# Hybrid encoder trunk: intra-chunk products in narrower column tiles, and reloads of spilled projections issued by SyncE

## The chip, the cores and the metric

The kernel runs on one core of one Trainium2 chip. The metric is the device time of one execution in microseconds (us). TensorE (PE) multiplies, VectorE (DVE) and ScalarE (ACT) read its results from PSUM, GpSimd (POOL) and SyncE (SP) do the rest. SP and ACT issue DMAs, each on a queue of its own.

## What is computed

Two layers of a bidirectional mixer over 512 + 256 tokens of width 1024, all in float32. Each layer has a gated linear attention branch (GLA, 4 heads, 128 channels for the key) and a grouped-query attention branch; both read one normalised input through one projection, are gated, projected, merged and projected again. The change touches the inner part of GLA. For one head and one direction it is

```python
def step(S, inp):
    qi, ki, vi, gi = inp
    b = jnp.cumsum(gi, axis=2)
    diff = b[:, :, :, None, :] - b[:, :, None, :, :]
    decay = jnp.exp(jnp.where(mask[None, None, :, :, None], diff, -jnp.inf))
    A = jnp.einsum('bhic,bhjc,bhijc->bhij', qi, ki, decay)
    o = (jnp.einsum('bhij,bhjv->bhiv', A, vi)
         + jnp.einsum('bhic,bhcv->bhiv', qi * jnp.exp(b), S))
```

with `g = log_sigmoid(h @ w_gate + b_gate) / 16`, run forward and, strictly, backward, and summed. The decay differs for each channel, so `A` isn't one product of two scaled matrices.

## The kernel before

**Levels.** The kernel builds the decayed token-by-token matrix of a head by doubling spans. `LEVELS` is 1, 2, 4 to 256. Step n = 0 gives the diagonal (no decay). Step n >= 1 has span `LEVELS[n - 1]`: it pairs each block of `span` tokens with its neighbour block, with queries and keys scaled by the decay to the border between the two. TensorE multiplies keys (stationary) by queries (moving) into PSUM, VectorE copies the entries that belong to this level into `amat` under a mask (`collect`, L1712; for n = 0 a plain copy of everything, L1710), and scales queries, keys and block totals for the next span (`doubled`, L1696, L1698, L1702). ScalarE merges the two scaled rows of keys into one (`merge_k`, L1064). An entry outside the mask of a level is never read from that level. A head has ten steps, n = 0 to 9; there are four heads in each of two layers, so eight heads in all.

**Shape of the products.** Steps 1 to 6 (spans 1 to 32) run as 12 matmuls of 64 by 64 at L733, each writing half of PSUM's partitions; steps 0, 7 and 8 run as six of 128 by 128 at L728; step 9 as four at L716. All are plain float32, and the trace shows each of them as two MATMUL rows (12 for six matmuls, 24 for twelve).

**What fills the time between.** While VectorE and ScalarE work on a level, TensorE runs `background`: the input projection of the columns that are needed later, three float32r matmuls (L585 to L587) for each token tile and k block, so many tiles for each step by the table `GLA_DONE` (mostly 11 tiles, 33 matmuls). Every finished 256-column group is copied by ScalarE to `stg` (L956) and stored to DRAM (`proj`, L973), 18 groups in each layer. Each matmul with w_hi and w_lo needs a weight block that SP has loaded (L493), that ScalarE has rounded (`split`, L941) and GpSimd has subtracted (L1431), in a ring of four slots. ScalarE's split stays three blocks ahead of TensorE, and SP's load one block further.

**Heads.** On TensorE the first three heads of a layer are one hardware loop (`at.repeat`), whose waits compare with register values and whose n = 0 product has a computed address; the fourth is written out.

**Reloads.** The stored groups come back by DMAs that ScalarE issues between its own work (`fetch`, L982), each 768 KB: in the fourth head one `q` or `kv` group in each step (`fetch_qk`), each followed one step later by ScalarE's squares of it (L1086); after the attention groups four of `zb` and four of `ma`; later four of `mb`. ScalarE's program is in order, so what stands behind an issue waits until the issue is over. `zb` and `ma` take the place of `act_lo` and `act_hi`, which the last background products read.

Of the kernel before, what the change touches and what calls it, by code (L numbers as in the profile page):

```python
# [58 lines left out]
CHUNK = 64  # L59
AH, KVH, DH = 16, 4, 64  # L60
# [55 lines left out]
for done, n in zip(ATT_DONE, ATT_PIECE):  # L116
# [22 lines left out]
        "w_lo_done": 8},  # L139
    "sync gla background": {  # L140
        "w_lo_done": 16},
    "sync rope background": {
        "w_lo_done": 8},
    "sync attention background": {
        "w_lo_done": 16},
    "sync gla branch": {
        "w_lo_done": 8},
    "sync attention branch": {
        "w_lo_done": 8},
# [76 lines left out]
class Semaphores:  # L226


    def __init__(self, nc):
# [21 lines left out]
        self.qkv_in = sem("qkv_in")  # L251
# [80 lines left out]
def trunk(nc, x_prompt, x_sample, norm_g, w_in, w_gate_f, b_gate_f, w_gate_b, b_gate_b, gla_norm_g,  # L332
# [139 lines left out]
    with nc.Block() as block:  # L472

        @block.sync
        def _(sp):
            at = Counts("sync", sp)
# [10 lines left out]
            def load_group(w, layer, col, width=HALF, blocks=KT):  # L487
                ld = w.shape[2]
                for k in range(blocks):

                    sp.wait_ge(s.w_lo_done, at("w_lo_done"))
                    src = bass.AP(w.tensor, layer * (D * ld) + col + k * P * ld, [[ld, P], [1, width]])
                    sp.dma_start(w_raw[:, k % RING, 0:width], src).then_inc(s.w_slot[k % RING], 16)  # L493

            def load_output(layer):

                for _ in range(2):
                    for i in range(2 * KT):
                        sp.wait_ge(s.w_lo_done, at("w_lo_done"))
                        src = bass.AP(w_out.tensor, layer * (D * D) + i % 2 * HALF + i // 2 * P * D, [[D, P], [1, HALF]])  # L500
                        sp.dma_start(w_raw[:, i % RING, :], src).then_inc(s.w_slot[i % RING], 16)

            for layer in range(DEPTH):
# [6 lines left out]
                with at.repeat(GH, "gla background") as h:  # L510
                    for i in range(2):
                        load_group(w_in, layer, h * (2 * BGW) + C_QB + BGW + i * BGW, BGW)
                load_group(w_in, layer, C_ZB + 3 * BGW, BGW)
# [5 lines left out]
                for w, name in ((w_branch_a, "gla branch"), (w_branch_b, "attention branch")):  # L519
                    with at.repeat(2, name) as g:  # L520
                        load_group(w, layer, g * HALF)
# [12 lines left out]
        def _(pe):  # L534
# [169 lines left out]
            def gla_levels(h, done, more):  # L704
                for n in range(GLA_STEPS):
# [12 lines left out]
                    elif n == 0 or span >= CHUNK:  # L718
                        for j in range(NT):
                            lhs = scaled[:, 4, j * P:(j + 1) * P]  # L720
                            if n == 0:
                                rhs = view(qk_t, h * (2 * TOK) + j * P, (1, P))
                            elif span == 128:
                                i = j ^ 1
                                rhs = scaled[:, j % 2, i * P:(i + 1) * P]
                            else:
                                rhs = view(scaled, TOK + j * P, (2 * span, P // (2 * span)), (span - TOK, 2), (1, span))
                            last = mm(ps[:, j * P:(j + 1) * P], lhs, rhs, start=True, stop=True)  # L728
                    else:
# [1299 lines left out]
```

## Time and profile before

| what | us |
|---|---|
| median of three runs (lowest, highest) | 1963.75 (1962.61, 1964.44) |
| profiled execution, its own time | 1963.97 |
| its span | 1962.2 |
| TensorE busy | 1907.5 |
| VectorE busy | 987.3 |
| ScalarE busy | 942.8 |
| GpSimd busy | 680.0 |

The times of the trace count from the start of the span; 1.8 us of the execution lie around it. PE counts matmuls and PEld the weight loads, which overlap them. Matmuls overlap one another too, so a row's duration is a latency; the distance between starts is what one costs. The share of an engine says little by itself; what matters is where TensorE stands still, and how long a step's products keep the background products waiting.

### The profile page before, as it was taken

The page shows a single profiled execution, that of the slowest core. Times are in us where ns is not written, and L with a number is a line of the kernel's source. Part 1 is how long each engine was busy: PE and PEld are TensorE (multiplying, and loading weights), DVE is VectorE, ACT ScalarE, POOL GpSimd, SP SyncE. Part 2 cuts the span into 40 slices and gives each one's busy share as a digit, 9 for nine tenths or more (in the row PEclk, how much of TensorE's full clock was granted, in tenths as well). Part 3 has the DMA queues.
Part 4 walks back from the last instruction along what each step waited for, and adds up shares of the span by engine and source line. Part 5 has one row for each costly group of instructions (what it writes and reads, how often), then busy time and mean ns, then how long its engine had stood idle before and what let it go on. Part 6 is the DMA issues. An engine that isn't in the chain of part 4 may idle for free.

```text
span 1962.2 us, 36081 instructions
## 1 busy us (share of the span) xinstructions
PE 1907.5 (97%) x13520; PEld 1754.9 (89%) x13520; DVE 987.3 (50%) x1376; ACT 942.8 (48%) x1891; POOL 680.0 (35%) x688
## 2 busy tenths in 40 slices
PE   6999999999999999999999999999999999999997
PEld 6989999999999998888899899999999999978886
DVE  5113556669655553433240145557786655643324
ACT  4214545533767765523441344554337776653334
POOL 3433133258312112323653323222771222132244
PEclk9999999999999999999999999999999999999999
DMA  5321221522112115242432122125221122162324
GB/s 174 86 57 58 68 75 59 171 84 60 54 47 66 47 49 179 92 129 69 134 107 65 48 75 61 62 69 182 76 54 49 47 66 65 56 195 65 120 94 141
DMA packets 122963, 169.48 MB, mean 86 GB/s; under 512 B 15696, under 2 KB 89296, under 8 KB 122832
## 3 DMA queue, kind: packets, MB, share of 16 engines
q1 hardware_dynamic: 82656, 107.52, 19.0%
q10 hardware_dynamic: 40176, 60.18, 9.0%
q8 instruction: 87, 1.43, 0.3%
q14 instruction: 44, 0.36, 0.1%
HBM read 136.19 MB, written 31.46 MB: 85 GB/s over the span
## 4 chain that ended last, share of the span: by engine, by line
PE 88%; DVE 4%; ACT 3%; issue 3%; ACTq 1%; DMA 0%; POOL 0%; DVEq 0%
PE ps L585 12%; PE ps L586 11%; PE ps L587 11%; PE ps L539 11%; PE ps L541 10%; PE ps L540 10%; PE ps L748 4%; PE ps L787 3%; PE ps L669 2%; PE ps L801 2%; PE ps L802 2%; PE ps L733 2%; PE ps L776 2%; PE ps L728 2%; PE ps L777 2%
## 5 line engine op out<-in xcount | busy, mean ns | idle before, releaser
L1431 POOL TENSOR_TENSOR w_lo<-w_raw,w_hi 128x256 fp32r<-128x256 f32 (+1 forms) x560 | 577.3, 1037 | 1238.3 <-ACT w_hi L941 1237.3
L585 PE MATMUL ps<-w_hi,act_hi 128*128 128x256 f32 x2112 | 610.2, 289 | 3.8 <-ACT stg L956 2.5
L587 PE MATMUL ps<-w_hi,act_lo 128*128 128x256 f32 x2112 | 597.1, 283 | 0.0
L586 PE MATMUL ps<-w_lo,act_hi 128*128 128x256 f32 x2112 | 597.1, 283 | 0.0
L941 ACT ACTIVATE w_hi<-w_raw 128x256 fp32r<-128x256 f32 (+1 forms) x560 | 273.4, 495 | 513.6 <-PE ps L541 287.0
L585 PEld LDWEIGHTS ps<-w_hi,act_hi 128*128 128x128 f32 x2112 | 403.8, 191 | 12.4 <-issue 4.1
L586 PEld LDWEIGHTS ps<-w_lo,act_hi 128*128 128x128 f32 x2112 | 404.5, 192 | 2.2
L587 PEld LDWEIGHTS ps<-w_hi,act_lo 128*128 128x128 f32 x2112 | 404.1, 191 | 0.0
L1838 DVE TENSOR_REDUCE st<-ps 128x1 f32<-128x512 f32 (+1 forms) x160 | 109.9, 691 | 126.6 <-PE ps L777 126.0
L539 PE MATMUL ps<-w_hi,o_hi 128*128 128x512 f32 x384 | 155.8, 406 | 1.7 <-DVE merged L1760 0.5
L541 PE MATMUL ps<-w_hi,o_lo 128*128 128x512 f32 x384 | 151.3, 394 | 0.0
L540 PE MATMUL ps<-w_lo,o_hi 128*128 128x512 f32 x384 | 150.9, 393 | 0.0
L1150 ACT ACTIVATE pr<-ps,st 128x512 f32<-128x512 f32 (+1 forms) x192 | 117.1, 612 | 11.8 <-DVE st L1838 9.5
L1844 DVE TENSOR_TENSOR pt_lo<-ps,pt_hi 128x512 fp32r<-128x512 f32 x128 | 88.2, 689 | 60.5 <-ACT pt_hi L1160 59.2
L1064 ACT ACTIVATE scaled<-scaled 128x768 f32<-128x768 f32 x64 | 53.2, 832 | 132.4 <-DVE scaled L1696 132.4
L1160 ACT ACTIVATE pt_hi<-ps 128x512 fp32r<-128x512 f32 x128 | 76.5, 598 | 66.6 <-PE ps L802 51.9
L787 PE MATMUL ps<-ident,pr 128*128 128x128 f32 x640 | 96.6, 273 | 7.7 <-DVE q_hl L1829 6.9
L1712 DVE COPY_PREDICATED amat<-mask,ps 128x768 f32<-128x768 uint8 x56 | 58.1, 1037 | 71.1 <-issue 56.1
L539 PEld LDWEIGHTS ps<-w_hi,o_hi 128*128 128x128 f32 x384 | 73.0, 190 | 19.2 <-issue 3.6
L541 PEld LDWEIGHTS ps<-w_hi,o_lo 128*128 128x128 f32 x384 | 72.8, 190 | 15.9
L539 PE MATMUL ps<-act_hi,w_hi 128*128 128x384 f32 x256 | 86.2, 337 | 0.6 <-DVE qk_t L1641 0.6
L541 PE MATMUL ps<-act_hi,w_lo 128*128 128x384 f32 x256 | 85.6, 334 | 0.0
(183 smaller groups left out, 3436.8 us busy)
## 6 DMA issues: line engine op xcount, KB each, us to landing
w_raw<-in_w_in SPq DMA_DIRECT2D x352, 128.0 KB, 2.1
proj<-stg ACTq DMA_DIRECT2D x36, 768.0 KB, 3.4
w_raw<-in_w_in SPq DMA_DIRECT2D x80, 256.0 KB, 2.7
w_raw<-in_w_out SPq DMA_DIRECT2D x64, 256.0 KB, 2.7
w_raw<-in_w_branch_a SPq DMA_DIRECT2D x32, 256.0 KB, 2.8
w_raw<-in_w_branch_b SPq DMA_DIRECT2D x32, 256.0 KB, 2.8
q<-proj ACTq DMA_DIRECT2D x8, 768.0 KB, 5.6
zb<-proj ACTq DMA_DIRECT2D x8, 768.0 KB, 10.1
```

Of the source, the lines that this page charges most:

```text
L539: mm(out, s_hi, m_hi, start=first, stop=False)
L540: mm(out, s_hi, m_lo, start=False, stop=False)
L541: return mm(out, s_lo, m_hi, start=False, stop=last)
L585: mm(out, act_hi[:, k, tok], w_hi[:, k % RING, 0:BGW], start=(k == 0 and t % 2 == 0), stop=False, skip_group_check=True)
L586: mm(out, act_hi[:, k, tok], w_lo[:, k % RING, 0:BGW], start=False, stop=False, skip_group_check=True)
L587: last = mm(out, act_lo[:, k, tok], w_hi[:, k % RING, 0:BGW], start=False, stop=(k == KT - 1), skip_group_check=True)
L787: last = nc.tensor.transpose(bank(pt_bank(n))[:, place * P:(place + 1) * P], pr[:, n % 2, j * P:(j + 1) * P], ident[:])
L941: A(w_hi[:, slot, 0:width], w_raw[:, slot, 0:width], ACT.Copy).then_inc(s.w_hi_done, 1)
L1150: last = A(pr[:, n % 2, i * w:(i + 1) * w], ps[:, n % 2 * HALF + i * w:n % 2 * HALF + (i + 1) * w], ACT.Exp, bias=nmax(n, i), accum_out=de ...
L1431: G.tensor_tensor(w_lo[:, slot, 0:width], w_raw[:, slot, 0:width], w_hi[:, slot, 0:width].bitcast(F32), ALU.subtract).then_inc(s.w_lo_done, 1)
L1838: V.tensor_reduce(out, view_ps(n % 2 * HALF, (HALF // k, k), (1, HALF // k)), AX.X, ALU.max, negate=True).then_inc(s.neg_max, 1)
L1844: V.tensor_tensor(p_turned(n, True), src, p_turned(n, False).bitcast(F32), ALU.subtract).then_inc(s.pt_lo_ready, 1)
```

## The change

1. Steps 0 to 5 (n = 0 and spans 1 to 16) become 24 matmuls of 32 by 32, each writing 32 partitions of PSUM, the four quarters in turn. Step 6 stays at 12 of 64 by 64. Step 7 (span 64) becomes 12 of 64 by 64 that compute the off-diagonal blocks alone. Steps 8 and 9 stay.
2. TensorE's first three heads are written out, not looped, so that their waits compare with constants.
3. All reloads move from ScalarE to SP, between the weight loads. `q` and `kv` start once the fourth head's first totals are there, one after each of the weight loads of the next blocks, with a semaphore for each group. `zb` starts after weight block 3 of `w_branch_a`, when TensorE has used the last background block; `ma` after block 8, when all 18 stores have landed; `mb` after block 8 of `w_branch_b`, when VectorE has made all gated products. The weight loads behind these waits in SP's program wait with them.

```diff
+QUARTER = 32
...
+            def fetch_inputs(layer, c):
+                if c == 0:
+                    sp.wait_ge(s.totals, (layer * GH + GH - 1) * NMASK + 1)
+                    sp.wait_ge(s.stored, at.peek("stored", 6 * 16))
+                if c < 4:
+                    fetch(q, J_Q + c, c * BGW, D, s.qkv_in[c])
+                else:
+                    fetch(kv, J_K + c - 4, (c - 4) * BGW, HALF, s.qkv_in[c])
+            def fetch_zb(k):
+                if k == 3:
+                    sp.wait_ge(s.w_used, at.peek("w_used", -4))
+                    sp.wait_ge(s.stored, at.peek("stored", 10 * 16))
+                if k >= 3 and k < 7:
+                    fetch(zb, J_ZB + k - 3, (k - 3) * BGW, D, s.zb_in)
+            def fetch_ma(k):
+                if k == 0:
+                    sp.wait_ge(s.stored, at.peek("stored", NBG * 16))
+                if k < 4:
+                    fetch(ma, J_MA + k, k * BGW, D, s.m_in[k // 2])
+            def fetch_mb(layer, k):
+                if k == 0:
+                    sp.wait_ge(s.b_gated, (layer + 1) * 2 * NT)
+                if k < 4:
+                    fetch(mb, J_MB + k, k * BGW, D, s.m_in[k // 2])
...
+                load_group(w_branch_a, layer, 0, between=fetch_zb)
+                load_group(w_branch_a, layer, HALF, between=fetch_ma)
+                load_group(w_branch_b, layer, 0)
+                load_group(w_branch_b, layer, HALF, between=lambda k: fetch_mb(layer, k))
...
-                    elif n == 0 or span >= CHUNK:
+                    elif span == 128:
                         for j in range(NT):
-                            lhs = scaled[:, 4, j * P:(j + 1) * P]
+                            i = j ^ 1
+                            last = mm(ps[:, j * P:(j + 1) * P], scaled[:, 4, j * P:(j + 1) * P],
+                                      scaled[:, j % 2, i * P:(i + 1) * P], start=True, stop=True)
+                    else:
+                        chunk = QUARTER if span < QUARTER else CHUNK
+                        for c in range(0, TOK, chunk):
+                            to = c
                             if n == 0:
-                                rhs = view(qk_t, h * (2 * TOK) + j * P, (1, P))
...
+                                rhs = view(qk_t, h * (2 * TOK) + c, (1, chunk))
+                            elif span == CHUNK:
+                                to = c ^ CHUNK
+                                rhs = scaled[:, c // CHUNK % 2, to:to + chunk]
                             else:
...
+                                rhs = view(scaled, TOK + c, (2 * span, chunk // (2 * span)), (span - TOK, 2), (1, span))
+                            last = mm(ps[c % P:c % P + chunk, to:to + chunk], scaled[:, 4, c:c + chunk], rhs, start=True, stop=True)
...
-                with at.repeat(GH - 1, "gla head") as h:
+                for h in range(GH - 1):
                     gla_levels(h, GLA_DONE, True)
...
-                if 1 <= n < 5:
-                    fetch(q, J_Q + n - 1, (n - 1) * BGW, D, 1, s.qkv_in)
-                if 5 <= n < 7:
-                    fetch(kv, J_K + n - 5, (n - 5) * BGW, HALF, 1, s.qkv_in)
...
-                for c in range(4):
-                    fetch(zb, J_ZB + c, c * BGW, D, 1, s.zb_in)
                 for k in range(KT):
                     split(k)
-                    if k < 2:
-                        fetch(ma, J_MA + k, k * BGW, D, 1, s.m_in[0])
```

The order of the instructions shows two of these places. First TensorE in a looped head, at step 1: a register instruction for each wait, the twelve products, a register instruction of the next background tile, and its products (lines 585 to 587). Before:

```order
L706 REGISTER_ALU
L733 MATMUL ps<-scaled 64x64 x12
L580 REGISTER_ALU
L585 MATMUL ps<-w_hi,act_hi 128x256
L586 MATMUL ps<-w_lo,act_hi 128x256
L587 MATMUL ps<-w_hi,act_lo 128x256
```

The same place with the change (the background products are lines 635 to 637 there):

```order
L637 MATMUL ps<-w_hi,act_lo 128x256
L784 MATMUL ps<-scaled 32x32 x24
L635 MATMUL ps<-w_hi,act_hi 128x256
L636 MATMUL ps<-w_lo,act_hi 128x256
L637 MATMUL ps<-w_hi,act_lo 128x256
```

The twelve matmuls have become 24, and the register instructions around them are gone.

Second ScalarE behind the last attention group: the last copies of background sums to `stg` and their store, then the reloads, the split of weight block 3 and the first copies of transposed tiles (`o_hi`). Before:

```order
L956 ACTIVATE stg<-ps 128x512 x3
L973 DMA proj<-stg 128x1536
L982 DMA zb<-proj 128x6x256 x4
L941 ACTIVATE w_hi<-w_raw 128x512
L982 DMA ma<-proj 128x6x256
L1004 ACTIVATE o_hi<-ps 128x4x128 x2
L941 ACTIVATE w_hi<-w_raw 128x512
```

The same place with the change:

```order
L1007 ACTIVATE stg<-ps 128x512 x3
L1024 DMA proj<-stg 128x1536
L992 ACTIVATE w_hi<-w_raw 128x512
L1049 ACTIVATE o_hi<-ps 128x4x128 x2
L992 ACTIVATE w_hi<-w_raw 128x512
```

The reloads that stood ahead of the split are gone from ScalarE. On SP they now stand between the weight loads of `w_branch_a`:

```order
L527 DMA w_raw<-in_w_branch_a 128x512 x4
L486 DMA zb<-proj 128x6x256
L527 DMA w_raw<-in_w_branch_a 128x512
L486 DMA zb<-proj 128x6x256
L527 DMA w_raw<-in_w_branch_a 128x512
```

Four weight blocks are loaded ahead of the first of them, and each later block stands behind a reload.

## Rows read from the trace of the kernel before

**Rows 1.** The page's head and its first part, TensorE's busy time.
```profile
span 1962.2 us, 36081 instructions
PE 1907.5 (97%) x13520; PEld 1754.9 (89%) x13520; DVE 987.3 (50%) x1376; ACT 942.8 (48%) x1891; POOL 680.0 (35%) x688
```

**Rows 2.** TensorE's waits: waiting line, releaser, us in total, times, longest.
```profile
PE ps L669 <- DVE o_lo L1595: 8.5, 2, 4.7
...
PE ps L585 <- ACT stg L956: 2.5, 8, 0.3
PE ps L728 <- issue: 2.4, 2, 1.2
```

**Rows 3.** Line 733 alone: duration ns (min, median, max), first and last start.
```profile
L733 PE MATMUL ps<-scaled x1152: 222/222/288, 184.8 to 1347.3; 128*64 128x64 f32 x192
```

**Rows 4.** TensorE in time, a step 1 and a step 2: start, duration, instruction.
```profile
241.33 1.22 PE L733 MATMUL ps<-scaled 128*64 128x64 f32 x24
242.48 0.39 PE L585 MATMUL ps<-w_hi,act_hi 128*128 128x256 f32 x1
...
246.42 0.28 PE L587 MATMUL ps<-w_hi,act_lo 128*128 128x256 f32 x1
246.63 0.97 PE L733 MATMUL ps<-scaled 128*64 128x64 f32 x24
247.52 0.39 PE L585 MATMUL ps<-w_hi,act_hi 128*128 128x256 f32 x1
247.75 0.28 PE L586 MATMUL ps<-w_lo,act_hi 128*128 128x256 f32 x1
```

**Rows 5.** The same of a step 7, 128 columns wide.
```profile
272.18 0.28 PE L587 MATMUL ps<-w_hi,act_lo 128*128 128x256 f32 x1
272.30 1.50 PE L728 MATMUL ps<-scaled 128*128 128x128 f32 x12
273.56 0.36 PE L585 MATMUL ps<-w_hi,act_hi 128*128 128x256 f32 x1
```

**Rows 6.** VectorE's copy of step 0, then line 580 alone within 241.54 to 241.56.
```profile
240.10 0.96 DVE L1710 COPY amat<-ps 128x768 f32<-128x768 f32 x1 [8.51 <-PE ps L728]
...
L580 PEldq ALU_OP  x1: 32/32/32, 241.6 to 241.6; - x1
```

**Rows 7.** The fourth head, steps 6 and 7: ScalarE and TensorE in time.
```profile
383.53 1.46 ACT L1086 ACTIVATE ps<-q 128x1536 f32<-128x1536 f32 x1 [3.05 <-DMA q<-proj]
384.92 0.83 ACT L1064 ACTIVATE scaled<-scaled 128x768 f32<-128x768 f32 x1
385.84 1.58 PE L728 MATMUL ps<-scaled 128*128 128x128 f32 x12 [1.18 <-issue]
```

**Rows 8.** Busy time by engine over step 5 of the fourth head.
```profile
375.65:380.81 5.16, 5.06 (x61) 4.82 (x58) 4.55 (x5) 3.67 (x6) 0.57 (x1) 1.00 0.74 239
```

**Rows 9.** Behind the last attention group: ScalarE, then TensorE in both layers.
```profile
765.79 5.94 ACTq L982 DMA_DIRECT2D zb<-proj  x4
771.84 0.63 ACT L941 ACTIVATE w_hi<-w_raw 128x512 fp32r<-128x512 f32 x1 [6.47 <-issue]
774.96 0.63 ACT L941 ACTIVATE w_hi<-w_raw 128x512 fp32r<-128x512 f32 x1
...
775.37 1.11 PE L669 MATMUL ps<-ident,va 128*128 128x128 f32 x4 [3.78 <-DVE o_lo L1595]
...
1743.19 1.10 PE L669 MATMUL ps<-ident,va 128*128 128x128 f32 x4 [4.74 <-DVE o_lo L1595]
```

**Rows 10.** Two stretches: length, busy PE, PEld, DVE, ACT, POOL, granted clock, DMA share, GB/s.
```profile
775.37:780.68 5.31, 5.31 (x16) 4.33 (x17) 1.23 (x2) 0.82 (x2) 1.27 (x1) 0.50 1.10 353
1743.24:1746.66 3.42, 3.42 (x11) 2.83 (x12) 1.18 (x2) 0.77 (x2) 1.27 (x1) 0.50 1.09 356
```

**Rows 11.** SP's load of weight block 4 of w_branch_a; then the page's DMA part.
```profile
755.93 0.33 SPq L493 DMA_DIRECT2D w_raw<-in_w_branch_a  x1
...
w_raw<-in_w_branch_a SPq DMA_DIRECT2D x32, 256.0 KB, 2.8
```

More of the change, by code:

```diff
@@ L250, in __init__ @@
         self.va_normed = sem("va_normed")
-        self.qkv_in = sem("qkv_in")
+        self.qkv_in = [sem(f"qkv_in{i}") for i in range(6)]
         self.zb_in = sem("zb_in")
@@ L475, in _ @@
         def _(sp):
-            at = Counts("sync", sp)
+            at = Counts("sync", sp, w_used=RING, stored=16)
             def tile_of(prompt, sample, t):
@@ L485, in _, with fetch, load_group @@
                     sp.wait_ge(s.x_in[NH - 2], 16)
-            def load_group(w, layer, col, width=HALF, blocks=KT):
+            def fetch(dst, j, start, row, sem):
+                sp.dma_start(view(dst, start, (row, NT), (1, BGW)),
+                             bass.AP(proj, j * (NT * BGW), [[NBG * NT * BGW, P], [BGW, NT], [1, BGW]])).then_inc(sem, 16)
+            def fetch_inputs(layer, c):
[22 more added lines that the diff above has]
+                    fetch(mb, J_MB + k, k * BGW, D, s.m_in[k // 2])
+            def load_group(w, layer, col, width=HALF, blocks=KT, between=None):
                 ld = w.shape[2]
@@ L509, in _, with after_first, with_inputs @@
                 load_group(w_in, layer, C_QB, BGW)
-                with at.repeat(GH, "gla background") as h:
+                with at.repeat(GH - 1, "gla background") as h:
                     for i in range(2):
                         load_group(w_in, layer, h * (2 * BGW) + C_QB + BGW + i * BGW, BGW)
+                def after_first(k):
+                    if k == KT - 1:
+                        fetch_inputs(layer, 0)
+                def with_inputs(k):
+                    if k + 1 < 6:
+                        fetch_inputs(layer, k + 1)
+                load_group(w_in, layer, C_QB + BGW + (GH - 1) * 2 * BGW, BGW, between=after_first)
+                load_group(w_in, layer, C_QB + BGW + (GH - 1) * 2 * BGW + BGW, BGW, between=with_inputs)
                 load_group(w_in, layer, C_ZB + 3 * BGW, BGW)
@@ L518, in _ @@
                         load_group(w_in, layer, g * (2 * BGW) + C_MA + i * BGW, BGW)
-                for w, name in ((w_branch_a, "gla branch"), (w_branch_b, "attention branch")):
-                    with at.repeat(2, name) as g:
-                        load_group(w, layer, g * HALF)
+                load_group(w_branch_a, layer, 0, between=fetch_zb)
+                load_group(w_branch_a, layer, HALF, between=fetch_ma)
+                load_group(w_branch_b, layer, 0)
+                load_group(w_branch_b, layer, HALF, between=lambda k: fetch_mb(layer, k))
+                at.skip("stored", NBG * 16)
                 load_output(layer)
@@ L977, in all_stored @@
                 act.wait_ge(s.stored, at.peek("stored", 16))
-            def fetch(dst, j, start, row, n, sem):
-                for c in range(n):
-                    act.dma_start(view(dst, start + c * BGW, (row, NT), (1, BGW)),
-                                  bass.AP(proj, (j + c) * (NT * BGW), [[NBG * NT * BGW, P], [BGW, NT], [1, BGW]])).then_inc(sem, 16)
             def param(dst, src):
@@ L1473, in rope_swapped @@
                     pool.wait_ge(s.tables, at("tables"))
-                    pool.wait_ge(s.qkv_in, at("qkv_in", 6 * 16))
+                    for c in range(6):
+                        pool.wait_ge(s.qkv_in[c], at(f"qkv_in{c}", 16))
                 pool.wait_ge(s.rot2_free, at("rot2_free"))
```

39 lines of the change are left out of this document (11 added, 28 removed).

## The prediction, made before the changed kernel had run

> **What bounds the kernel now.** I read the page's first part, then TensorE's waits, then TensorE in time. TensorE is busy 1907.5 of 1962.2 us, VectorE and ScalarE about half [rows 1]. The share alone says only that something can be won in two ways: by closing the gaps where TensorE stands still, or by making its own work shorter where nothing else would then be late. The waits name the gaps that the change touches: 8.5 us in two places where it waits for `o_lo` (L669), 2.5 us for `stg`, and 2.4 us before L728 in two places [rows 2]. In the eight GLA heads TensorE has no other gap: background products fill the time between the levels, so the products of a level are simply added to the length of the step.
>
> **Part 1, the products of the levels.** In step 2 the last background product starts at 246.42, the level at 246.63, the next background product at 247.52 [rows 4]. Background products start 0.12 apart [272.18 to 272.30, rows 5], so entering costs 0.21 - 0.12 = 0.09 and the level itself 0.89. Its 24 rows span 0.97, of which the last takes 0.222 [rows 3]: twelve matmuls start within 0.75, 62 ns each, and 0.15 is left for leaving. Step 1 takes 241.33 to 242.48 = 1.15. A 128-wide level takes 272.30 to 273.56 = 1.26 without a cost of entering [rows 5], though it streams as many columns: the two halves of PSUM's partitions work side by side in the 64-wide form, two matmuls in 2 x 62 = 124 ns where one of twice the width and height takes 1.26 / 6 = 210.
>
> What 24 matmuls of 32 by 32 take is in no row, so I bound it. *From below*: four quarters side by side. A quarter streams half as many columns as a half does, so a group of four should take a little over half of what a group of two does; I take 70 ns for four matmuls where two take 124, hence 0.42 for 24, and 0.57 with the 0.15. *From the engine's queue*: something must hand 24 matmuls over instead of twelve. In step 1 of a looped head the level waits for VectorE's copy, which ends at 240.10 + 0.96 = 241.06, and the register instruction that stands behind the twelve matmuls (L580) runs at 241.55 [rows 6]. So twelve were handed over in at most 0.49, 41 ns each; less the time to take up the semaphore I use 38. 24 then need 0.91. The head start shortens this: in step 1 it is 241.33 - 241.06 = 0.27, so the level would last 0.91 - 0.27 + 0.15 = 0.79, against 1.15: 0.36 saved. In the other steps the release comes earlier and more is queued when the array gets there; I estimate nine matmuls (0.27 / 0.038 = 7 is the least), which leaves 15 x 0.038 + 0.15 = 0.72. *From above*: no gain in width (0.89), or worse, the rivals below. I take the middle case, 0.79 and 0.72, because the 41 ns is the row nearest to the question.
>
> The sum for one head: step 0, 1.26 - 0.72 - 0.09 for entering = 0.45; step 1, 0.36; steps 2 to 4, 3 x 0.17 = 0.51; step 6 nothing; step 7, which becomes 64-wide, 1.26 - 0.89 - 0.09 = 0.28; steps 8 and 9 nothing. Step 5 gives nothing in the first three heads of a layer: TensorE waits there for `stg`, 2.5 / 8 = 0.31 each [rows 2], at the end of a chain (VectorE, `merge_k`, gate magnitudes, copies to `stg`) that starts with the end of step 4, and what the level loses the wait gains. In the fourth head there are no gates, and its step 5 saves 0.17. So 1.60 for six heads and 1.77 for two: **13.1 us**. What is late next in the fourth head is VectorE, 4.55 busy in a step of 5.16 [rows 8]; a step that is 0.17 shorter still covers it.
>
> The Trainium skill speaks against the narrow form twice. "TensorEngine Tiling (Array Packing)", Instruction Overhead, says that a matmul has an overhead of about 60 cycles and that no tiling factor should be taken from a dimension that is already small; by it 32 moving columns cost what 60 do and the levels stay at 0.89. "TensorE: Matmul & The Clock Gate", section "Wait — 56ns, not 53.3ns?", gives about 62 ns for a MATMUL decoded by microcode as the bound of short ones; the equal spacing of step 2 could be just that. The rows say otherwise in part (41 ns at most for handing one over), and both are priced as rivals.
>
> **Part 2, heads written out.** It takes register instructions off TensorE's sequencer. They run while the array works on what is queued, and TensorE has no gap at them, so I cost them at nothing. If the longer code came late, a gap would show at the start of a head.
>
> **Part 3, q and kv by SP.** In the fourth head ScalarE waits 3.05 for a reload that it issued one step earlier, squares it until 384.99, and only then merges the keys (384.92 to 385.75) that TensorE's step 7 needs; TensorE idles 1.18 there [rows 7], 2.4 in both layers [rows 2]. With SP one reload follows each weight load, so this one is issued about two steps earlier, and the merge no longer stands behind a landing. Next late is the merge behind VectorE, which is earlier than TensorE's need. **2.4 us.** SP's wait for the totals holds no block back that is soon wanted, since a block is loaded one ring ahead of its split.
>
> **Part 3, zb and ma by SP.** ScalarE issues four reloads in 5.94, and its split behind them starts 6.47 late; the copies of `o_hi` wait behind that, then VectorE's `o_lo`, and TensorE stands 3.78 and 4.74 in the two layers [rows 9]. Behind each gap the granted clock is 0.50, 1.2 GHz, for 5.31 and 3.42 us, while TensorE is busy throughout [rows 10]; at full clock the work of these stretches takes half, so 2.65 + 1.71 = 4.4 us go with the gaps. Together 8.5 + 4.4 = **12.9 us**. The price sits on SP: weight block 4 was loaded at 755.93 [rows 11] and will now wait until TensorE has used the last background block, which is before ScalarE's issue at 765.79 [rows 9], say 765, so about 9 us, and it shares a queue with the reloads. A landing takes 2.8 alone [rows 11]; behind one 768 KB reload at 353 GB/s [rows 10], 2.2 us more, and an issue of 0.4, it is there at about 765 + 0.4 + 2.2 + 2.8 = 770.4. ScalarE's splits of blocks 3 and 4 were 774.96 - 771.84 = 3.1 apart [rows 9]; with the first at about 766 it wants block 4 at 769, and may wait some 1 us, little beside the 3.78. Blocks 5 to 7 follow at one reload each, faster than TensorE uses blocks. So I cost this at nothing; without that cover ScalarE waits at its split again, in program order, and the `o_hi` copies with it. `mb` has no gap before and none is expected.
>
> **The forecast.** 13.1 + 2.4 + 12.9 = 28.4 off the profiled execution's 1963.97 gives 1935.6. That execution lies 0.2 above the median and inside the runs' range, so the same number stands for the median.
>
> **The rivals.**
> *All four quarters at full speed* (0.57 in steps 0 to 5): step 0 saves 0.60, step 1 0.58, steps 2 to 4 0.96, step 7 0.28, 2.42 in a head and 0.32 more in the fourth, 20.0 in all; 1928.7. For it speaks that 41 ns is only an upper bound.
> *The width brings nothing*: levels stay at 0.89. Step 0 and step 7 save 0.28 each, 4.5 in all, with 15.3 from the reloads 1944.2. For it speaks step 1, slower than step 2 with the same products but for the pattern of the queries, 1.15 against 0.89: the reading of the moving operand may already be near its limit.
> *The reloads' gain is lost* because weights stand behind them on SP, in whole: 13.1 is left, 1950.9. Against it speaks the arithmetic of block 4, for it that the margin there is small.
> *Slower*: the 62 ns of step 2 is a price for each matmul, whatever its size. A 32-wide level then lasts 24 x 0.062 + 0.15 = 1.64. Step 0 costs 1.64 + 0.09 - 1.26 = 0.47 more, step 1 0.49, steps 2 to 4 2.25, step 5 0.75 less the 0.31 of waiting, step 7 saves 0.28: 3.37 in a head, 3.68 in a fourth, 27.6 in all, 12.3 more than the reloads give; 1976.3. The same sum with a price p is 1152 p - 43.9, which equals 15.3 at p = 51 ns: from there on it decides the sign. Against it stand the 41 ns.
> *The change doesn't do what it says*: the quarters are taken one after another. Then p is at or above that point too, and it goes with the slower case.
>
> **How the numbers follow.** Forecast 0.46, full speed 0.18, no gain from width 0.13, reloads lost 0.08, slower 0.13, within 0.2% 0.02 (about what a measurement of this kernel can tell from no change). The range from 1928 to 1951 takes in the first four, 0.85. Faster 0.85, same 0.02, slower 0.13.
>
> **What would show it.** In the changed profile: steps 2 to 4 from the level's first start to the next background product near 0.72 (0.57, 0.89 and 1.64 in the rivals), step 1 near 0.79, step 7 near 0.89; 48 MATMUL rows in each narrow level; no idle before step 7 of the fourth head; no `o_lo` wait at the first transposes of `va`, and no stretch of half clock behind it; the `stg` wait in step 5 longer than 0.31. I am wrong if a narrow level lasts longer than 24 x 0.051 + 0.15 = 1.37, or if ScalarE waits at the splits of blocks 4 to 7 of `w_branch_a`.

## The result and the profile after

| | before | after |
|---|---|---|
| median of four runs (lowest, highest), us | 1963.96 (1962.61, 1964.44) | 1932.95 (1931.96, 1933.88) |
| profiled execution, us | 1963.97 | 1933.38 |
| TensorE busy, us | 1907.5 | 1882.5 |

The changed kernel takes 0.9843 of the time of before (95% interval 0.9826 to 0.9860): 31.0 us less by the medians, where 28.4 had been forecast. The page's head, the engines' busy times, the granted clock in 40 slices and two lines on DMA:

```profile
span 1931.0 us, 38149 instructions
...
PE 1882.5 (97%) x14864; PEld 1728.9 (90%) x14864; DVE 987.7 (51%) x1376; ACT 944.0 (49%) x1891; POOL 682.8 (35%) x688
...
PEclk9999999999999999999999999999999999999999
...
q8 instruction: 113, 1.85, 0.4%
...
q<-proj SPq DMA_DIRECT2D x8, 768.0 KB, 8.8
```

A 9 stands for 90% or more of a slice of 48 us, and the page of before shows the same row, so short stretches of half clock don't show in it; the windows further down do. Queue q8 brings instructions in 113 packets of 16 KB, and a `q` reload lands 8.8 behind its issue (the median of eight), among SP's other transfers.

TensorE's waits, against [rows 2]. The line for `o_lo` is gone; the wait for `stg` has more than doubled; that ahead of the levels (L784, the levels up to 64 wide) is as long as it was, but is another one:

```profile
PE ps L635 <- ACT stg L1007: 5.3, 11, 0.7
...
PE ps L784 <- issue: 2.4, 3, 1.2
```

A narrow step 1 and step 2, against [rows 4] (start, duration, instruction). From the level's start to the next background product they take 184.81 - 184.16 = 0.65 and 189.52 - 188.96 = 0.56; before, 1.15 and 0.89:

```profile
184.16 0.71 PE L784 MATMUL ps<-scaled 128*32 128x32 f32 x48
184.81 0.39 PE L635 MATMUL ps<-w_hi,act_hi 128*128 128x256 f32 x1
188.96 0.63 PE L784 MATMUL ps<-scaled 128*32 128x32 f32 x48
189.52 0.39 PE L635 MATMUL ps<-w_hi,act_hi 128*128 128x256 f32 x1
```

Step 7, against [rows 5]: 269.02 - 268.17 = 0.85, where 1.26 stood:

```profile
268.17 0.92 PE L784 MATMUL ps<-scaled 128*64 128x64 f32 x24
269.02 0.39 PE L635 MATMUL ps<-w_hi,act_hi 128*128 128x256 f32 x1
```

Behind the last attention group, against [rows 9, 10]: ten microseconds from the first `zb` reload on (columns as in rows 10). TensorE is busy 9.93 of 10.00 at full clock, although ScalarE now waits 0.67 and 0.30 for weight blocks (ACT L992 is its split):

```profile
755.50:765.50 10.00, 9.93 (x52) 8.21 (x52) 2.08 (x3) 4.25 (x8) 3.67 (x3) 1.00 0.87 279
...
762.14 0.63 ACT L992 ACTIVATE w_hi<-w_raw 128x512 fp32r<-128x512 f32 x1 [0.67 <-DMA w_raw<-in_w_branch_a]
...
766.81 0.63 ACT L992 ACTIVATE w_hi<-w_raw 128x512 fp32r<-128x512 f32 x1 [0.30 <-DMA w_raw<-in_w_branch_a]
```

**Where the time went.** The length of each stage, from the first matmul of a stage to the first of the next, shows it without the noise of the other stages (us; where a layer's value differs, both stand). They come from one profiled execution of each kernel, and are the measure for the experiments below beside the medians.

| stage | before | after | change, both layers | forecast |
|---|---|---|---|---|
| heads 1 to 3 of a layer | 56.57 each | 54.58, 54.32, 54.32 | -13.0 | -9.6 |
| fourth head to the end of attention | 412.64, 412.68 | 410.64, 409.49 | -2.00 - 3.19 = -5.2 | -5.9 |
| first output product (`zb`, `ma` come in) | 78.51, 78.59 | 72.06, 72.06 | -13.0 | -12.9 |
| all others | | | within 0.2 | 0 |

Two terms of the forecast are wrong in opposite directions: ordinary heads give 2.25 where 1.60 was worked out (the first of a layer 1.99, mostly because TensorE waits 0.22 for `stg` behind its short step 0), and the fourth heads give 2.00 and 3.19 where 1.77 + 1.2 = 2.97 was worked out for each. Shorter levels alone would have given them more than that. TensorE stands still in them in places where it had not. The first is step 2 in both layers (here layer 0), the second is in the middle of the 48 rows of step 5, in layer 0 alone; a third, 0.22 for `stg` behind step 5 of layer 1 (at 1319.44), takes what that level gave there:

```profile
351.72 0.28 PE L637 MATMUL ps<-w_hi,act_lo 128*128 128x256 f32 x1
352.61 0.62 PE L784 MATMUL ps<-scaled 128*32 128x32 f32 x48 [0.61 <-issue]
...
366.72 0.56 PE L784 MATMUL ps<-scaled 128*32 128x32 f32 x40
368.44 0.27 PE L784 MATMUL ps<-scaled 128*32 128x32 f32 x8 [1.16 <-issue]
368.64 0.38 PE L635 MATMUL ps<-w_hi,act_hi 128*128 128x256 f32 x1
```

What stands ahead of the first on ScalarE (ACTq is an issue of a DMA): four small loads, then the merge of keys that step 2 needs:

```profile
349.69 0.36 ACTq L1031 DMA_DIRECT2D cs_raw<-in_rope_cos  x1
350.08 0.46 ACTq L1031 DMA_DIRECT2D cs_raw<-in_rope_sin  x1
350.57 0.45 ACTq L1031 DMA_DIRECT2D g_qk<-in_q_norm_g  x1
351.05 0.45 ACTq L1031 DMA_DIRECT2D g_qk<-in_k_norm_g  x1
351.55 0.96 ACT L1109 ACTIVATE scaled<-scaled 128x768 f32<-128x768 f32 x1 [1.46 <-issue]
```

### The profile page after: what moved, and what is told of

It is laid out like the page before. It is cut to its first block, busy times and chain, and to the rows that moved or that the text cites. A ratio compares the mean times of both kernels' runs of the same rounds, so it can differ in the third digit from the quotient of the medians.

```text
span 1931.0 us, 38149 instructions
## 1 busy us (share of the span) xinstructions
PE 1882.5 (97%) x14864; PEld 1728.9 (90%) x14864; DVE 987.7 (51%) x1376; ACT 944.0 (49%) x1891; POOL 682.8 (35%) x688
## 4 chain that ended last, share of the span: by engine, by line
PE 89%; DVE 4%; ACT 3%; issue 3%; ACTq 1%; DMA 0%; POOL 0%; DVEq 0%
PE ps L635 12%; PE ps L636 12%; PE ps L637 12%; PE ps L589 11%; PE ps L591 11%; PE ps L590 11%; PE ps L799 4%; PE ps L838 3%; PE ps L719 2%; PE ps L852 2%; PE ps L853 2%; PE ps L827 2%; PE ps L784 2%; PE ps L828 2%; PE ps L766 1%
## 5 line engine op out<-in xcount | busy, mean ns | idle before, releaser
L992 ACT ACTIVATE w_hi<-w_raw 128x256 fp32r<-128x256 f32 (+1 forms) x560 | 273.5, 495 | 507.2 <-PE ps L591 284.2
```

The source lines that it names most:

```text
L992: A(w_hi[:, slot, 0:width], w_raw[:, slot, 0:width], ACT.Copy).then_inc(s.w_hi_done, 1)
```

## The experiments

The median of before was 1964.29, 1964.34 and 1963.53 us beside the three groups of four.

### The two halves of the change apart

**levels_only** is the kernel before with the new shapes and the heads written out; the reloads stay on ScalarE.

> The kernel before with the narrow levels and the heads written out, reloads still issued by ScalarE. In the changed kernel a narrow level lasts 0.56 (0.65 in step 1) where 0.89 (1.15) stood, and the first three heads of a layer are 2.25 shorter each. Theory A, the two halves of the change add up: 6 x 2.25, 2 x 2.74 in the fourth heads, less 0.44 at the first step of each layer, 18.5 in all, 1945.4 us. Theory B, the reloads on ScalarE were timed to the old steps: the stall before step 7 of the fourth head (1.18) grows by what the levels give in the steps ahead of it, up to 2 us in each layer, so 1947 to 1949.4. Theory C, the wait of 0.61 before step 2 of the fourth head comes from SyncE's full queue: then it is absent here; if it comes from the shorter steps it is here too.

Measured: 1949.15 us, ratio 0.9924 (0.9907 to 0.9940). Heads 1 to 3 are as short as in the changed kernel (54.59, 54.33, 54.33), but the fourth stage is 415.14 and 411.72, so 2.5 longer and 1.0 shorter than before. Theory B holds: the median lies in its 1947 to 1949.4. The profiled execution, 1952.37, is the slowest of the four and lost more than that. The idle before step 2 is here as well (0.64 in each layer), so theory C's queue is not its cause. ScalarE in step 6 and TensorE's step 7 behind it, then a stretch of TensorE (length, busy PE, PEld, DVE, ACT, POOL, granted clock, DMA share, GB/s):

```profile
376.96 1.45 ACT L1088 ACTIVATE ps<-q 128x1536 f32<-128x1536 f32 x1 [4.09 <-DMA q<-proj]
378.35 0.83 ACT L1066 ACTIVATE scaled<-scaled 128x768 f32<-128x768 f32 x1
...
379.28 0.97 PE L735 MATMUL ps<-scaled 128*64 128x64 f32 x24 [2.22 <-issue]
...
380.18:383.50 3.32, 3.32 (x17) 3.32 (x16) 3.14 (x6) 1.88 (x2) 0.80 (x2) 0.51 0.55 142
```

ScalarE waits 4.09 for a reload issued one step ahead, merges the keys only then, TensorE idles 2.22, and for 3.3 us behind that the granted clock is 0.51, 1.2 GHz. Steps 5 and 6 of this head start late as well, by 0.95 and 0.80. Shorter steps leave a reload that is issued one step ahead less time to land.

**reloads_only** is the changed kernel with the old shapes and the loop:

```diff
-                    elif span == 128:
+                    elif n == 0 or span >= CHUNK:
...
-                        chunk = QUARTER if span < QUARTER else CHUNK
-                        for c in range(0, TOK, chunk):
+                        for c in range(0, TOK, CHUNK):
...
-                for h in range(GH - 1):
+                with at.repeat(GH - 1, "gla head") as h:
```

> The changed kernel with the old shapes of all levels and looped heads: only the reloads moved to SyncE. Theory A (as predicted): zb and ma give 13.0, q and kv 2.4 by the stall before step 7 of the fourth head: 1948.5. Theory B (the new stalls seen in the changed kernel's fourth head, 0.61 before step 2 and 1.16 inside step 5, belong to the reloads on SyncE and not to the narrow levels): they are here too, 13.0 + 2.4 - 1.2 - 1.4 = 12.8, 1951.2. Theory C (the stall inside step 5 is a late fetch of instructions, which the longer code of the written heads and 24 matmuls brings): it is absent here.

Measured: 1946.84 us, ratio 0.9913 (0.9897 to 0.9930). The output stage is 72.02 in both layers (-6.49, -6.57), the fourth stage 411.05 and 411.08 (-1.6 each, where 1.2 had been forecast), and no idle is left ahead of steps 2 to 7: theory A. The idle inside step 5 is absent, as C says, but that isn't a test of C's cause: it is absent as well in kernels below that have the narrow levels and the written heads.

Do the two halves add up? By the stages of these profiles the moved reloads are worth 1.6 in a fourth stage with the old shapes, and 415.14 - 410.64 = 4.5 and 411.72 - 409.49 = 2.2 with the new ones. But the 4.5 comes from the slowest execution of levels_only, 3.2 above its median. By the medians the levels give 15.1 and the reloads 17.5, 32.6 together, and the whole change gives 31.0 to 31.3, depending on the median of before. So it is not shown that one half makes the other pay more. What the profiles show is where the levels alone lose time: at reloads that land late.

### What sets the length of a narrow level

In both of these the 24 matmuls of a narrow level are the same, only their order changes; the first list is that of **quarter_order**, the second that of **quarter_pairs** (`c` is the column, `c % P` its place in PSUM's 128 partitions).

```diff
-                        for c in range(0, TOK, chunk):
+                        some = [c for r in range(0, P, chunk) for c in range(r, TOK, P)] if chunk == QUARTER else range(0, TOK, chunk)
...
+                        some = [c + i for r in range(0, P, CHUNK) for c in range(r, TOK, P) for i in (0, QUARTER)] if chunk == QUARTER else range(0, TOK, chunk)
...
+                        for c in some:
```

> The changed kernel with the same 24 matmuls of each narrow level in another order: six for the first quarter of PSUM's partitions, then six for the second, and so on. Theory A, the level is short because four neighbours with different quarters run side by side: with none side by side each takes the 62 ns of the old form, 24 x 0.062 + 0.15 = 1.64 in place of 0.56. Five steps 1.08 longer, step 5 by 1.08 less the 0.69 of its wait: 5.8 in a head, 6.5 in a fourth, 48 in all, 1981. Theory B, the matmuls are handed over and started at 17 ns each whatever quarter they use: 1933, no change.

Measured: 1964.73 us, the median of ten runs from 1963.43 to 1983.87, ratio 1.0014 (0.9993 to 1.0035). The total is that of the kernel before again: what the reloads gave, the levels now cost. Step 1 and step 2:

```profile
242.53 1.76 PE L785 MATMUL ps<-scaled 128*32 128x32 f32 x48
244.22 0.39 PE L635 MATMUL ps<-w_hi,act_hi 128*128 128x256 f32 x1
...
248.37 1.45 PE L785 MATMUL ps<-scaled 128*32 128x32 f32 x48
249.75 0.39 PE L635 MATMUL ps<-w_hi,act_hi 128*128 128x256 f32 x1
```

Step 2 takes 1.38, so (1.38 - 0.15) / 24 = 51 ns for a matmul against 17 with four quarters in turn. Theory A, with 51 ns in place of 62; heads 2 and 3 are 58.54 (+4.2). Since 51 ns is the break-even price of the prediction's slower rival, the tie with the kernel before is what its sum gives.

The 51 ns is a mean over an order that changes quarters three times. Of the level's rows (line 785 alone), 40 have started by 249.36 and 47 by 249.60:

```profile
248.37:249.36 0.99, 0.99 (x40) 0.99 (x41) 1.00 0.08 17
248.37:249.60 1.23, 1.23 (x47) 1.23 (x48) 1.00 0.07 13
```

In this last stretch one quarter works alone, and its rows start 0.24 / 7 = 34 ns apart, 68 ns for a matmul of two rows. At that price 24 would take 1.6; that the level is shorter says that matmuls overlap where the quarter changes. In the changed kernel a quarter does its twelve rows in 0.41, again 34 ns for each. So in this step a quarter is as fast beside three others as alone, and four of them do four times the work.

> The changed kernel with the 24 matmuls of a narrow level in pairs of quarters: the first and second quarter in turn, twelve of them, then the third and fourth. One quarter at a time took 1.34 to 1.38 (50 ns for each matmul), all four in turn 0.56 (17 ns). Theory A, two side by side halve the price: 24 x 0.025 + 0.15 = 0.75, 0.19 more in five steps of eight heads and nothing in step 5 but the fourth heads': 8 us more, 1941. Theory B, it is enough that two matmuls in a row use different quarters: 0.56, no change.

Measured: 1939.22 us, ratio 0.9882 (0.9866 to 0.9898).

```profile
243.40 0.87 PE L785 MATMUL ps<-scaled 128*32 128x32 f32 x48
244.20 0.39 PE L635 MATMUL ps<-w_hi,act_hi 128*128 128x256 f32 x1
```

0.80, so 27 ns for a matmul, and heads 2 and 3 are 55.61: theory A. Orders with one, two and four quarters in turn give 51, 27 and 17 ns.

**wide_moving** keeps the order and doubles the moving columns:

```diff
-                                rhs = view(qk_t, h * (2 * TOK) + c, (1, chunk))
+                                to = c // CHUNK * CHUNK
+                                rhs = view(qk_t, h * (2 * TOK) + to, (1, CHUNK))
...
-                                rhs = view(scaled, TOK + c, (2 * span, chunk // (2 * span)), (span - TOK, 2), (1, span))
-                            last = mm(ps[c % P:c % P + chunk, to:to + chunk], scaled[:, 4, c:c + chunk], rhs, start=True, stop=True)
+                                to = c // CHUNK * CHUNK
+                                rhs = view(scaled, TOK + to, (2 * span, CHUNK // (2 * span)), (span - TOK, 2), (1, span))
+                            last = mm(ps[c % P:c % P + chunk, to:to + CHUNK], scaled[:, 4, c:c + chunk], rhs, start=True, stop=True)
```

> The changed kernel with 64 moving columns for each of the 24 matmuls of a narrow level (32 by 64; the extra entries are overwritten or never read). Theory A, a level lasts as long as its columns take with four quarters side by side: 24 x 64 / 4 is what 12 x 64 / 2 was, so 0.89 again, 0.33 more in steps 0 to 4, nothing in step 5 of heads 1 to 3 (its wait shrinks), 0.33 in the fourth: 13.9 in all, 1946.9. Theory B, a matmul of this size costs a fixed 17 ns (0.41 / 24): 1933, no change.

Measured: 1942.58 us, ratio 0.9891 (0.9874 to 0.9907).

```profile
239.70 1.23 PE L786 MATMUL ps<-scaled 128*32 128x64 f32 x48
240.85 0.38 PE L635 MATMUL ps<-w_hi,act_hi 128*128 128x256 f32 x1
...
244.99 0.94 PE L786 MATMUL ps<-scaled 128*32 128x64 f32 x48
245.87 0.39 PE L635 MATMUL ps<-w_hi,act_hi 128*128 128x256 f32 x1
```

Step 2 is 0.88 and step 1 is 1.15, as with twelve of 64 by 64 (0.89 and 1.15) [rows 4]: theory A. 24 matmuls can be handed over in far less than the prediction's 38 ns each (0.41 / 24 = 17 in the changed kernel), and what they stream sets the time. The total is 4.3 us under the 1946.9 expected: TensorE no longer idles 0.61 + 1.16 + 0.61 in the fourth heads, and steps 3 and 4 take 0.81, not 0.89.

### The new losses in the fourth head

**params_sp**: the four small loads leave ScalarE and stand on SP behind the reloads.

```diff
-                    param(cs_raw[:, 0, :, :], rope_cos)
-                    param(cs_raw[:, 1, :, :], rope_sin)
-                    param(g_qk[:, 0, :], rows_of(q_norm_g, layer * DH, DH))
-                    param(g_qk[:, 1, :], rows_of(k_norm_g, layer * DH, DH))
...
+                    sp.dma_start(dst, src).then_inc(s.param, 16)
```

> The changed kernel with the four small loads of rope tables and norm weights (1.8 us of issues in front of merge_k in step 1 of the fourth head) issued by SyncE behind its reloads. Theory A, those issues are why the keys of step 2 come 0.61 late there: the idle before step 2 is gone in both layers, the fourth heads are 0.6 shorter each, 1.2 in all. Theory B, VectorE's scaling is late in any case: the idle stays at 0.3 or more. The stall of 1.16 inside step 5 should stay by both.

Measured: 1930.10 us, ratio 0.9826 (0.9810 to 0.9843). Step 2 starts 0.21 behind the last background product, without idle:

```profile
350.16 0.28 PE L640 MATMUL ps<-w_hi,act_lo 128*128 128x256 f32 x1
350.37 0.63 PE L787 MATMUL ps<-scaled 128*32 128x32 f32 x48
```

Theory A for step 2: the fourth stage of layer 1 is 408.81 (-0.68). But the idle inside step 5 is gone too (408.82 in layer 0), against both theories, although the reloads still stand behind every weight block.

**reloads_spaced**:

```diff
-                    if k + 1 < 6:
-                        fetch_inputs(layer, k + 1)
+                    if k % 2:
+                        fetch_inputs(layer, (k + 1) // 2)
```

The sixth stands behind the second block of the next group.

> The changed kernel with the q and kv reloads on SyncE behind every second weight block instead of every one. Theory A, the idle of 1.16 inside step 5 of the first layer's fourth head is a fetch of instructions that waits behind the reloads in the DMA engines (350 GB/s then): with half the traffic it is gone or below 0.3, 1.1 less in all. Theory B, it depends on the place in the code alone: it stays near 1.2 at the same instruction. Theory C, the reloads now land too late for ScalarE's squares, which stand ahead of merge_k, and the stalls before steps 3 to 7 come back with 1 to 3 us in a layer.

Measured: 1932.30 us, ratio 0.9836 (0.9819 to 0.9852). The median is within what a measurement can tell from the changed kernel's; the stages are clearer: the idle of 1.16 is gone (409.35, -1.3), that of 0.6 before step 2 stays, layer 1 is 409.46. The DMA of 359 to 365.8 us in this kernel; then, in the changed kernel, the same stretch and the one behind it (queue, kind: packets, MB, share of 16 engines):

```profile
q1 hardware_dynamic: 1814, 1.76, 86.0%
q8 instruction: 1, 0.02, 1.0%
```

```profile
q1 hardware_dynamic: 2456, 2.42, 109.6%
...
q1 hardware_dynamic: 947, 0.94, 107.1%
q8 instruction: 1, 0.02, 2.7%
```

With the reloads spaced, a 16 KB packet of instructions comes within that stretch (at 362.79 in the trace, 5.5 behind the one before it). With a reload behind every weight block the DMA engines are full for the whole of it, SP's queue moves some 350 GB/s, and the packet comes at 365.90, 8.6 behind the one before it; TensorE stops at 367.3. That fits theory A, a fetch of instructions that is late behind the reloads. No view names who waits for the packet, and TensorE resumes at 368.44, some time after it.

Other kernels speak against it. These are the stretches from one such packet to the next in the changed kernel, params_sp and step0_wide:

```profile
357.27:365.90 8.63, 8.63 (x157) 8.38 (x157) 7.80 (x10) 5.46 (x7) 2.20 (x3) 1.00 1.07 350
...
360.03:368.45 8.42, 8.20 (x150) 7.95 (x136) 8.24 (x11) 5.98 (x8) 1.47 (x2) 1.00 1.11 353
...
356.03:366.91 10.88, 10.88 (x177) 10.53 (x176) 9.36 (x12) 6.52 (x9) 2.94 (x4) 1.00 1.06 336
```

The traffic is much the same and the packets are about as far apart or farther, but in the last two TensorE never stands still inside a level. So neither the traffic nor the distance of the packets is enough to bring the idle, and its cause stays open.

**step6_quarters** makes step 6 narrow as well, of the blocks off the diagonal:

```diff
-                        chunk = QUARTER if span < QUARTER else CHUNK
+                        chunk = QUARTER if span < CHUNK else CHUNK
...
-                            elif span == CHUNK:
-                                to = c ^ CHUNK
-                                rhs = scaled[:, c // CHUNK % 2, to:to + chunk]
+                            elif span == chunk:
+                                to = c ^ span
+                                rhs = scaled[:, c // span % 2, to:to + chunk]
```

> The changed kernel with step 6 (span 32) in 24 matmuls of 32 by 32 as well, of the blocks off the diagonal alone. It lasts 0.85 and should last 0.56. Theory A, nothing else is late then: 0.29 in each of eight heads, 2.3 in all. Theory B, VectorE or ScalarE is late behind it by now, as in step 2 of the fourth head and in step 5: 0 to 1.2 in all, and an idle before step 7 or 8 shows who is late.

Measured: 1930.50 us, ratio 0.9822 (0.9805 to 0.9838). Step 6 takes 0.56, heads 2 and 3 are 54.02 (-0.30): theory A. In the fourth head of layer 0 the long idle has moved. It is 0.97 now, and stands at another instruction, in step 4, ahead of a background product that waits for nothing new:

```profile
361.62 0.39 PE L635 MATMUL ps<-w_hi,act_hi 128*128 128x256 f32 x1
362.97 0.28 PE L636 MATMUL ps<-w_lo,act_hi 128*128 128x256 f32 x1 [0.97 <-issue]
```

Here the packet of instructions comes at 360.43, 13.1 us behind the one before it (at 347.31), with SP's queue at 350 GB/s from 354 on. That an idle with no wait in the program again follows a packet that came late speaks for the late fetch; params_sp and step0_wide speak against it, and no run decides.

**best_sp** joins the three edits.

> The three edits together: small loads on SyncE, reloads behind every second block, step 6 in quarters. If they are independent: 1.2 + 1.1 + 2.3 = 4.6 less than the changed kernel. If a shorter step only exposes the next late engine, less than 2.3.

Measured: 1928.18 us, ratio 0.9815 (0.9799 to 0.9831), 4.8 less than the changed kernel. The stages are 54.29, 54.02 and 54.02 for the heads, 408.52 and 408.53 for the fourth. The sum of 4.6 comes out, but not because the edits are independent. Alone they gave 2.85, 0.65 and 2.45 by the medians, 5.95 together. Params_sp and reloads_spaced each remove the idle inside step 5, which counts once. Beside params_sp the spacing brings nothing that the stages show: its fourth stage of 408.82 is here shorter by 0.30, and that is the narrow step 6.

**best_defer** adds one for heads 1 to 3: ScalarE's last split of step 4 goes behind the copies to `stg`.

```diff
-                        store(2 * h + 1)
+                        after_store = [i for i in start if start[i] == 4 and more]
+                        store(2 * h + 1, later=len(after_store))
+                        for i in after_store:
+                            split(i, BGW)
...
-                        if start[i] == n:
+                        if start[i] == n and not (more and n == 4):
```

> The kernel with the three edits together (best_sp), and in the first three heads of a layer ScalarE's split of step 4 moved behind the copies to stg of step 5. In the changed kernel that split stands from 258.38 to 258.69 ahead of the first copy, while TensorE waits 0.69 for it. Theory A, the wait is ScalarE's order alone: it falls by 0.31 to 0.38 in each of six heads, 1.9 less than best_sp. Theory B, the split's block is then late for TensorE, or VectorE is: the gain is lost at step 6 or 7.

Measured: 1925.27 us, ratio 0.9808 (0.9791 to 0.9824), the fastest kernel of this study and faster than the changed one by 7.7 us. Theory A: the wait falls from 0.69 to 0.39, heads 2 and 3 to 53.71. The stages give 1.9 less than best_sp, as expected, the medians 2.9. ScalarE and TensorE around it:

```profile
254.62 1.67 ACT L1082 ACTIVATE gate<-ps,bg_fix 128x768 f32<-128x768 f32 x2
256.19 1.57 ACT L1010 ACTIVATE stg<-ps 128x512 f32<-128x512 f32 x3
...
255.91 0.63 PE L787 MATMUL ps<-scaled 128*32 128x32 f32 x48
256.93 0.35 PE L638 MATMUL ps<-w_hi,act_hi 128*128 128x256 f32 x1 [0.39 <-ACT stg L1010]
```

The rest of the wait is behind the two gate magnitudes; to move one of them was not tried.

### Heads written out

**step0_wide** and **loops_kept** differ in this alone; step 0 is at 128 by 128 in both.

```diff
-                for h in range(GH - 1):
+                with at.repeat(GH - 1, "gla head") as h:
```

> The changed kernel with step 0 alone back at six matmuls of 128 by 128, heads written out. Step 0 took 1.26 so and 0.56 in the changed kernel: 0.70 in each of eight heads, 5.6 in all, 1938.5. It is the base for the next kernel.

> The same (step 0 at 128 by 128) with the first three heads of a layer as a loop, as before. Theory A, writing the heads out neither costs nor gives anything: heads and total within 0.5 us of step0_wide. Theory B, the register instructions ahead of each step are in the path once the levels are short: up to 0.1 in each of ten steps, 6 us in six heads. Theory C, the written heads cost instruction fetches: the loop is faster by 0.5 or more.

Measured: 1934.35 us (0.9851, 0.9835 to 0.9867) and 1934.59 us (0.9854, 0.9838 to 0.9871). Theory A of the second holds for the total: the packets of instructions go from 111 to 91, the looped heads are 54.84 where the written ones are 54.90, and the time is the same. The first missed: it is 4 us faster than expected. The narrow step 0 gives 54.90 - 54.32 = 0.58 in heads 2 and 3, not 0.70, only 0.32 in the first head of a layer, where the wait for `stg` takes the rest, and in the fourth heads it costs 1.0 in sum: with the longer step 0 ScalarE is on time for step 2 and no idle stands inside step 5 (409.51 and 409.57 against 410.64 and 409.49).

## Why the prediction was right, and where it was wrong

**Reloads of zb and ma: right.** 12.9 forecast, 13.0 measured, and the mechanism as told: no idle, no half clock there. Block 4 landed at 762.12, 6.6 us behind the first reload's issue at 755.53, where 0.4 + 2.2 + 2.8 = 5.4 had been worked out. The check "wrong if ScalarE waits at the splits" was set too strictly. ScalarE does wait there, and its slack covers it.

**q and kv: the stall went, the list of what is late next was wrong.** The merge before step 7 is on time, as forecast; by reloads_only that is worth 1.6 in each layer, not 1.2. But "what is late next" was asked of steps 6 and 7 only. In step 2 ScalarE had been in time by 0.5 before (the merge ended at 359.27, the step began at 359.77); steps 0 and 1, shorter by 0.58 + 0.50, made it late by 0.6. Step 5 of the fourth head was to save 0.17, and saved nothing: the copy to `stg` is late there too, by 0.22. The idle of 1.16 inside step 5 of layer 0 was not foreseen either. A reload behind every weight block fills the DMA engines for some 15 us there (share 1.07 from 355 to 370); whether that brings the idle is open.

**The levels: right in mechanism, wrong in size.** The failing step is "from the engine's queue": 38 ns for each matmul, taken as the rate because its row was the nearest. The row gave an upper bound, 0.49 for the hand-over of twelve; it said nothing of how much faster the sequencer could be. The bound from below, 0.42 + 0.15 = 0.57, was the right value: 0.56 measured. The rival at full speed was close: 0.58 in step 0 where it had 0.60, 0.50 in step 1 (0.58), 0.33 in step 2 (0.32), 2.25 in a head (2.42). (Steps 3 and 4 had taken 0.85 before, not the 0.89 of step 2, so they gave 0.29 each.) That rival's total of 1928.7 did not come either, because of the losses in the fourth heads. It is in part luck that the total lies only 2.6 us from the forecast. Heads 1 to 3 gave 3.4 more than worked out. The fourth heads would have given more as well, but idles of 0.61, 0.61 and 1.16, 2.4 us that are in no term of the prediction, took it back. Wide_moving is the test that would have settled it: twice the columns, no more instructions, and the old length is back.

The Trainium skill, "TensorEngine Tiling (Array Packing)", Instruction Overhead, counts about 60 cycles for each matmul. A plain float32 product is two rows of the trace here, and with one quarter at a time 1.23 us for 48 rows are 26 ns each, 61 cycles at 2.4 GHz. That is near the page's figure, but it is a mean: where one quarter works alone it is 34 ns, about 82 cycles. With four quarters in turn it is 0.41 / 48 = 8.5 ns, so the overhead of neighbours overlaps, and the advice drawn from it would have left this gain unused. The 62 ns of "TensorE: Matmul & The Clock Gate", section "Wait — 56ns, not 53.3ns?", limit nothing here.

**Step 5** of heads 1 to 3 behaved as told: the `stg` wait took what the level gave, 0.33 before and 0.69 after. **Heads written out** cost nothing, as told. **The slower rival** had its mechanism right: it describes quarter_order, where the price of 51 ns and a time equal to before's were measured together. What kept it away is the order in which the quarters take turns.

## What to carry to other kernels

Small matmuls on quarters of PSUM's partitions paid here only where neighbours in the program use different quarters; measure the price with the order changed and with the columns doubled, which separates overlap, hand-over and streaming in two runs. When every step of a pipeline gets shorter, ask of each other engine, in each kind of step, how much slack it had, and look at those that were just in time: a DMA issue ahead of the one instruction that others wait for, a reload that is issued exactly one step ahead. Large transfers on one queue can be spread as far as their readers allow: here that took 1.3 us off one stage by itself, and nothing beside another edit that had removed the same idle. When edits are joined, compare the stages and not only the sum, for two of them may have removed the same thing.

## What the runs showed of the hardware that was not expected

- Orders with one, two and four quarters in turn: 51, 27 and 17 ns for a 32 by 32 float32 matmul on average, and with 64 columns and four quarters (0.88 - 0.15) / 24 = 30 ns. In step 2 a quarter starts a row every 34 ns, alone or beside three others.
- The interleaved pattern of the queries in step 1 costs more the fewer quarters work side by side: over step 2 it adds 1.69 - 1.38 = 0.31 with one, 0.19 with two (0.99 against 0.80) and 0.09 with four.
- TensorE can stop in the middle of a level, between matmuls that wait for nothing: 1.16 us in the changed kernel. In step6_quarters it stops for 0.97 between two background products. In both the DMA engines were full with reloads; kernels with the same traffic had no such idle, and the cause is not shown.
- One early stage, between the first products of the gates, lasted 24.0 us in some profiled executions (before, the changed kernel) and 22.5 in others (levels_only, best_sp), whatever the kernel. Two spans can differ by 1.5 us for that alone, which is why stages were compared. The granted clock goes with it. The same stretch of the changed kernel, then of best_sp:

```profile
20.20:22.80 2.60, 2.60 (x10) 2.60 (x10) 0.00 (x0) 2.60 (x9) 2.56 (x3) 0.50 0.46 110
...
20.20:22.80 2.60, 2.60 (x17) 2.60 (x16) 0.52 (x1) 2.60 (x10) 2.50 (x2) 1.00 0.48 117
```

In the changed kernel it is 0.50, 1.2 GHz, and TensorE has 10 products in the stretch; in best_sp it is 1.00, with 17. TensorE had stood still before both, 2.07 and 1.73 us.
